# Splitting a norm by token halves between two matmul stages of a decoder layer

## The reference

```
h = h + mod[:, 1, 2] * (merged @ w_out)
u = rms_norm(h, gn[2]) * (1 + scale) + shift
h = h + 0.5 * mod[:, 2, 2] * ((silu(gate(u)) * val(u)) @ w_ffn2_down)
```

## Time and profile before

| | us |
|---|---|
| median of 3 runs | 1338.77 |
| lowest, highest | 1338.13, 1339.8 |
| the profiled execution's own time | 1338.71 |
| its span, first to last instruction | 1336.9 |
| PE busy | 1307.4 (98%) |
| DVE busy | 807.5 (60%) |
| ACT busy | 560.5 (42%) |
| POOL busy | 130.3 (10%) |
| mean granted TensorE clock | 0.994 of full speed |

### The profile page before, as it was taken

How to read it: one execution, slowest core, us unless ns; L and a number is a source line. 1 busy time by engine, 2 the same in 40 slices (tenths; PEclk the granted TensorE clock), 3 DMA queues, 4 the chain that set the end, 5 groups by cost and what they waited for, 6 DMA issues and landing times.

```text
span 1336.9 us, 26512 instructions
## 1 busy us (share of the span) xinstructions
PE 1307.4 (98%) x10448; PEld 1219.0 (91%) x10448; DVE 807.5 (60%) x1665; ACT 560.5 (42%) x1101; POOL 130.3 (10%) x144
## 2 busy tenths in 40 slices
PE   7899999999999999999999999999999999999997
PEld 5698888999999989999898687899899999999997
DVE  4549686789622254446546645553698888973334
ACT  1255454566511143223236545542466555651213
POOL 2320000000011120000003210033300000001110
PEclk9899999999999999999999999999999999999999
DMA  9922877322344346354572221073123222233332
GB/s 341 367 104 64 286 261 252 114 98 95 112 154 153 90 170 199 114 185 134 143 262 88 95 73 39 25 214 111 48 80 110 96 95 96 95 109 88 87 86 78
DMA packets 98772, 180.90 MB, mean 135 GB/s; under 512 B 14005, under 2 KB 49461, under 8 KB 97502
## 3 DMA queue, kind: packets, MB, share of 16 engines
q1 hardware_dynamic: 89734, 163.81, 38.0%
q10 hardware_dynamic: 8920, 15.46, 3.2%
HBM read 173.11 MB, written 10.28 MB: 137 GB/s over the span
## 4 chain that ended last, share of the span: by engine, by line
PE 87%; SPq 4%; DVE 3%; DMA 2%; issue 2%; ACT 1%; ACTq 1%; POOL 0%; DVEq 0%; POOLq 0%
PE PS L2405 31%; PE PS L2481 31%; PE PS L2791 7%; PE PS L2437 3%; PE PS L2292 3%; PE PS L2805 2%; PE PS L2354 2%; PE PS L2817 2%; PE PS L2833 2%; SPq L838 1%; PE PS L2600 1%; DMA raw<-in_w_gu 1%; ACTq L1037 1%; DMA raw<-in_w_in 1%; DMA ch<-in_cmp_pages 1%
## 5 line engine op out<-in xcount | busy, mean ns | idle before, releaser
L2481 PE MATMUL PS<-X,wh 128*128 128x272 f32 x2240 | 428.2, 290 | 1.3 <-DVE wl L1672 0.8
L2481 PEld LDWEIGHTS PS<-X,wh 128*128 128x128 f32 x2240 | 352.0, 188 | 16.3 <-issue 12.7
L2481 PE MATMUL PS<-X,wl 128*128 128x272 f32 x1120 | 324.2, 289 | 0.0
L1566 DVE TENSOR_TENSOR wl<-raw,wh 128x1024 fp32r<-128x1024 f32 (+3 forms) x127 | 133.7, 1054 | 237.4 <-ACT wh L1086 237.1
L1086 ACT ACTIVATE wh<-raw 128x1024 fp32r<-128x1024 f32 (+3 forms) x125 | 110.1, 882 | 349.8 <-PE PS L2405 330.1
L2481 PEld LDWEIGHTS PS<-X,wl 128*128 128x128 f32 x1120 | 210.7, 188 | 0.0
L2405 PE MATMUL PS<-hl,wh 128*128 128x272 f32 x660 | 136.1, 288 | 0.0
L1149 ACT ACTIVATE wh<-S 128x512 fp32r<-128x512 f32 x160 | 100.5, 628 | 63.9 <-DVE S L1691 34.6
L1672 DVE TENSOR_TENSOR wl<-S,wh 128x512 fp32r<-128x512 f32 x160 | 109.9, 687 | 26.6 <-ACT wh L1149 26.3
L2405 PEld LDWEIGHTS PS<-hl,wh 128*128 128x128 f32 x660 | 103.6, 188 | 0.0
L2405 PE MATMUL PS<-X,wh 128*128 128x272 f32 x518 | 102.1, 288 | 0.0
(11 more groups left out here) (386 smaller groups left out, 2360.2 us busy)
## 6 DMA issues: line engine op xcount, KB each, us to landing
raw<-in_w_gu SPq DMA_DIRECT2D x88, 512.0 KB, 4.3
ada<-in_w_ada SPq DMA_DIRECT2D x24, 1024.0 KB, 5.5
raw<-in_w_in SPq DMA_DIRECT2D x39, 512.0 KB, 4.2
raw<-in_w_dn SPq DMA_DIRECT2D x32, 384.0 KB, 3.2
raw<-in_w_dn SPq DMA_DIRECT2D x32, 320.0 KB, 2.9
ada<-in_w_ada ACTq DMA_DIRECT2D x8, 1024.0 KB, 11.4
ch<-in_cmp_pages SPq DMA_DIRECT2D x56, 128.0 KB, 6.3
kv<-in_sel_pages SPq DMA_DIRECT2D x112, 64.0 KB, 1.9
```

Of the source, the lines that this page charges most:

```text
L1566: e.tensor_tensor(wl[:, u % SPLITS, 0:n, :], raw[:, u % RAWS, 0:n, :], f(wh[:, u % SPLITS, 0:n, :]), ALU.subtract).then_inc(lo_ready, 1)
L2481: ins = mm(triple(i, PASS_BANK[j]), w[:, k, :], X[:, s, part, k, :], start=(j in (A11, A12, S1) and k == 0 and w is wh_ and part == 0), st ...
```

## The change: what it does

- Output tiles 6 and 7 run by halves: 6 a=0, 7 a=0, 6 a=1, 7 a=1, 24 matmuls each. DVE adds each half to `h` when it is done (`residual_half`); POOL squares tile 6 by halves, ACT tile 7.
- The norm's sum, root, diagonal and spread exist once per half. The first half's sums stand on PE inside tile 6's second half (before k=4), its spread inside tile 7's second half (before k=2).
- The pair of gate units takes all eight k of half 0, then all of half 1, and waits for `u_lo` before each. Half 1's sums stand behind k=1 of half 0, its spread behind k=4; the eight `ada_step`s follow k=2 to 7 of half 0.
- The pair's weights go to tiles of their own, `wh_ahead` and `wl_ahead`, split by ACT and DVE ahead of the norm. Unit ug+2 is split whole, at the norm's end, and no longer in two parts.
- Semaphore counts behind the norm are shifted. SP's list is as it was.

The diff, cut to its core:

```diff
-PAIRS = (U_GU1, U_WIN, U_CO, U_GU2)
+PAIRS = (U_GU1, U_WIN, U_CO)
...
+        s8 = ExitStack()
+        sb(s8, "in_use_8", [P, 4 * T])
+        wh_ahead = sb(s8, "wh_ahead", [P, 2, 8, P], F32R)
+        wl_ahead = sb(s8, "wl_ahead", [P, 2, 8, P], F32R)
+        s8.close()
...
-                with e.Fori(0, KD - 1) as k:
+                with e.Fori(0, KD - 2 if n == 2 else KD - 1) as k:
...
+                if n == 2:
+                    for a in range(2):
+                        e.wait_ge(h_ready, 2 * KD - 1 + 2 * a)
+                        e.wait_ge(ssq_ready, 23 + a)
+                        e.tensor_tensor(sq[:, side(a)], h[:, KD - 2, side(a)], h[:, KD - 2, side(a)], ALU.mult
+                                        ).then_inc(sq_ready, 1)
+                        e.wait_ge(sq_ready, 21 + a)
+                        e.tensor_tensor(ssq[:, side(a)], ssq[:, side(a)], sq[:, side(a)], ALU.add).then_inc(ssq_ready, 1)
...
+            def split_ahead(u):
+
+                e.wait_ge(raw_in[u % RAWS], 16 * (u // RAWS + 1))
+                e.wait_ge(unit_used, U_OUT)
+                e.activation(wh_ahead[:, u - U_GU2, :, :], raw[:, u % RAWS, :, :], ACT.Copy).then_inc(hi_ready, 1)
+
+            def norm_halves():
+
+                def squared(a):
+                    e.wait_ge(h_ready, 16 + 2 * a)
+                    e.activation(rinv[:, side(a)], h[:, KD - 1, side(a)], ACT.Square).then_inc(sq_last, 1)
+
+                def rooted(a):
+                    e.wait_ge(ms_ready, 3 + a)
+                    e.activation(root5[:, 3 * a:3 * a + 3], root5[:, 3 * a:3 * a + 3], ACT.Sqrt).then_inc(root_ready, 1)
+
+                def modulated(a, k):
+                    e.wait_ge(nt_ready, 16 + KD * a + k + 1)
+                    t0, t1 = HT * a, TP if a else HT
+                    e.activation(normed(2, k)[:, t0:t1], normed(2, k)[:, t0:t1], ACT.Identity,
+                                 scale=mods[:, 48 + 8 + k, 0:1], bias=mods[:, 48 + k, 0:1]).then_inc(nt_mod, 1)
+
+                def rounded(a, k):
+                    e.wait_ge(nt_mod, 16 + KD * a + k + 1)
+                    if a:
+                        e.wait_ge(ns_mod, 16 + k + 1)
+                    e.activation(X[:, x_set(k, a), 0, k % 4, :], normed(2, k)[:, side(a)], ACT.Copy).then_inc(u_hi, 1)
+
+                squared(0)
+                rooted(0)
+                e.wait_ge(mods_ready, 3)
+                for a in range(2):
+                    for k in range(KD):
+                        modulated(a, k)
+                        if k == 0:
+                            rounded(a, 0)
+                        elif k > 1:
+                            rounded(a, k - 1)
+                        if (a, k) == (0, 2):
+                            squared(1)
+                        elif (a, k) == (0, 3):
+                            rooted(1)
+                    rounded(a, KD - 1)
+                u = U_GU2 + 2
+                e.wait_ge(raw_in[u % RAWS], 16 * (u // RAWS + 1))
+                e.wait_ge(unit_used, U_OUT + KD - 1)
+                e.activation(wh[:, u % SPLITS, :, :], raw[:, u % RAWS, :, :], ACT.Copy).then_inc(hi_ready, 1)
...
-                split_second(ug + 2)
+                if n == 0:
+                    split_second(ug + 2)
...
-                split(u)
+                if u < U_GU2:
+                    split(u)
+                else:
+                    split_ahead(u)
...
-            norm(2)
+            norm_halves()
...
+            def norm_halves():
+
+                def lo_ahead(u):
+                    e.wait_ge(hi_ready, u + 1)
+                    e.tensor_tensor(wl_ahead[:, u - U_GU2, :, :], raw[:, u % RAWS, :, :], f(wh_ahead[:, u - U_GU2, :, :]),
+                                    ALU.subtract).then_inc(lo_ready, 1)
+
+                def residual_half(m, a):
+                    o = PS[:, 2 * (m % 4) + a, 0:HT]
+                    gm = mods[:, 24 + 16 + m, :]
+                    if a == 0:
+                        e.wait_ge(half_used, m - KD + 3)
+                        e.scalar_tensor_tensor(out=h[:, m, 0:HT], in0=o, scalar=gm[:, 0:1], in1=h[:, m, 0:HT],
+                                               op0=ALU.mult, op1=ALU.add).then_inc(h_ready, 1)
+                        return
+                    e.wait_ge(unit_used, U_OUT + m + 1)
+                    e.scalar_tensor_tensor(out=h[:, m, HT:TP], in0=o[:, 0:PA], scalar=gm[:, 0:1], in1=h[:, m, HT:TP],
+                                           op0=ALU.mult, op1=ALU.add)
+                    e.tensor_tensor(sres[:, :].rearrange("p (b q) -> p b q", b=NB),
+                                    o[:, PA:HT].rearrange("p (b q) -> p b q", b=NB),
+                                    gm[:, 1:NMOD].unsqueeze(2).broadcast_to([P, NB, SQ]), ALU.mult).then_inc(psum_free, 1)
+                    e.wait_ge(psum_free, O_OUT + m + 1)
+                    e.tensor_tensor(h[:, m, TP:T], h[:, m, TP:T], sres[:, :], ALU.add).then_inc(h_ready, 1)
+                    e.wait_ge(h_ready, 2 * KD + m - KD + 3)
+
+                def factors(a):
+                    r3 = root5[:, 3 * a:3 * a + 3]
+                    e.wait_ge(ssum_ready, 3 + a)
+                    e.tensor_scalar(r3, PS[:, 4, 4 * a:4 * a + 3], 1.0 / D, EPS, ALU.mult, ALU.add).then_inc(ms_ready, 1)
+                    e.wait_ge(root_ready, 3 + a)
+                    e.reciprocal(r3, r3).then_inc(rinv_ready, 1)
+                    e.wait_ge(rinv_ready, 3 + a)
+                    e.tensor_tensor(rinv[:, HT * a:HT * a + 2 * P].rearrange("p (t q) -> p t q", t=2),
+                                    ident.unsqueeze(1).broadcast_to([P, 2, P]),
+                                    r3[:, 0:2].unsqueeze(2).broadcast_to([P, 2, P]), ALU.mult)
+                    e.tensor_scalar(rinv[:, HT * a + 2 * P:HT * a + HT], ident[:, 3 * P - HT:P], r3[:, 2:3], None, ALU.mult
+                                    ).then_inc(diag_ready, 1)
+
+                def scaled(a, k):
+                    if k == 0:
+                        e.wait_ge(spread_ready, 5 + a)
+                    e.tensor_tensor(normed(2, k)[:, side(a)], h[:, k, side(a)], PS[:, 6 + a, 0:HT], ALU.mult
+                                    ).then_inc(nt_ready, 1)
+
+                def low(a, k):
+                    e.wait_ge(u_hi, 16 + KD * a + k + 1)
+                    s = x_set(k, a)
+                    e.tensor_tensor(X[:, s, 1, k % 4, :], normed(2, k)[:, side(a)], f(X[:, s, 0, k % 4, :]), ALU.subtract
+                                    ).then_inc(u_lo, 1)
+
+                lo_ahead(U_GU2)
+                residual_half(KD - 2, 0)
+                lo_ahead(U_GU2 + 1)
+                residual_half(KD - 1, 0)
+                factors(0)
+                residual_half(KD - 2, 1)
+                for a in range(2):
+                    scaled(a, 0)
+                    scaled(a, 1)
+                    for k in range(KD):
+                        if k + 2 < KD:
+                            scaled(a, k + 2)
+                        if (a, k) == (0, 1):
+                            residual_half(KD - 1, 1)
+                        elif (a, k) == (0, 3):
+                            factors(1)
+                        low(a, k)
+                lo(U_GU2 + 2)
...
-            for m in range(KD):
-                if m < KD - 1:
-                    lo(U_OUT + m + 2)
+            for m in range(KD - 2):
+                lo(U_OUT + m + 2)
                 e.wait_ge(unit_used, U_OUT + m + 1)
                 residual(m, 0, 24 + 16, m % 4, O_OUT, KD)
-            lo(U_OUT + KD + 1)
-            norm(2)
+            norm_halves()
...
+            def norm_halves():
+
+                def sums(tile, a, first):
+                    for t, c in enumerate((0, P, HT - P)):
+                        ins = mm(PS[:, 4, 4 * a + t:4 * a + t + 1], tile[:, HT * a + c:HT * a + c + P], ones[:, 0:1],
+                                 start=(first and t == 0), stop=not first, skip_group_check=True)
+                    return ins
+
+                def squares_summed(a):
+                    e.wait_ge(ssq_ready, 24 + a)
+                    sums(ssq, a, True)
+                    e.wait_ge(sq_last, 3 + a)
+                    sums(rinv, a, False).then_inc(ssum_ready, 1)
+
+                def spread(a):
+                    e.wait_ge(diag_ready, 5 + a)
+                    mm(PS[:, 6 + a, 0:HT], ones[:, :], rinv[:, side(a)], start=True, stop=True).then_inc(spread_ready, 1)
+
+                def output_half(m, a, at):
+                    u = U_OUT + m
+                    if a == 0:
+                        e.wait_ge(lo_ready, u + 1)
+                        e.wait_ge(psum_free, O_OUT + m - 3)
+                    for k in range(KD):
+                        if k in at:
+                            at[k](0)
+                        for w, x in ((wh, mh), (wh, ml), (wl, mh)):
+                            ins = mm(PS[:, 2 * (m % 4) + a, 0:HT], w[:, u % SPLITS, k, :], x[:, k, side(a)],
```

(85 more changed lines are left out.)

29 lines of the change are left out of this document (15 added, 14 removed).

## The result

The changed kernel takes 1342.03 us (median of 13 runs, 1340.35 to 1344.76) against 1338.73 for the kernel before, run beside it (13 runs, 1336.48 to 1340.31): ratio 1.0027, interval 1.0019 to 1.0035. It is slower by 3.3 us. The forecast was +0.7, in the class "within 0.2%", with 1341.9 as the upper end. The profiled execution took 1342.66, with a span of 1340.9 (before: 1336.9) and a mean granted clock of 0.992 (before: 0.994).

A forecast was written before the change was run, and what follows sets the result against it. PE was taken as the bound, so only its standing still around the third norm could be won. Stalls 3.4 against 2.6 (+0.8), sums +0.5, Strassen gap -0.6: net +0.7 us, 1339.4, range 1337.4 to 1341.9.

The forecast's parts named there:

- The collision and the stall: Before the first half's sums: DVE's subtractions and POOL's squares and additions block each other, so PE stands still 2.2 us.
- all three hand-overs: Between DVE and POOL before `ssq`: second begins 0.14 before the first ends; by the skill's figure each is 0.25 us later.
- The mixture in the pair: In the pair of gate units: 64 rows of `ada_step` priced about 4.0 us, wide matmuls 0.75 per k.
- The pair's waits: PE's waits: 0.1 at the pair's first k, 0.8 at k=1, 0.2 at k=3, 0.1 behind the last k.
- The sums: One-column sums of the norm: 24 rows for 20, +0.5 us of PE work.
- The gap in the Strassen part: Behind unit ug+3: PE's wait for DVE's product L1785, 0.4 us or 0.6 by turns, disappears: -0.6.
- POOL is not in the way: Rival, before the first sums: `ssq` ready at 942.8, first stall only 0.4, 1.8 less, 1337.6 us; chance 0.12.
- everything hides: Rival: all PE's stalls (2.6 + 0.6) are won, less 0.5 for sums: 1336.0 us at best; chance 0.03.
- The samples on POOL hold the second half: Rival, pair's second half: ACT's rounding waits for POOL's operations, PE loses time, +2.5, in all 1341.9 us; chance 0.12.

The follow-up runs named there:

- the filled kernel: Sixteen wide matmuls with unread results put on PE ahead of the wait for the first half's squares, on the changed kernel: 1340.61 us, ratio 1.0017.
- the runs with four groups instead of six: The eight `ada_step`s in four pairs, their sum copied before the split, on the kernel with tile 5's residual first and sums one k later: 1337.30 us, ratio 0.9984.
- the one with two groups: The changed kernel with its eight `ada_step`s in two groups of four, behind k=2 and k=3: 1342.74 us, ratio 1.0034.
- that with stall and sums apart: The changed kernel with the wait for the squares left at k=4 and the first half's sums moved to k=7: 1343.30 us, ratio 1.0031.
- the kernel with later sums: The changed kernel with tile 5's residual ahead of tile 7's weight split and the first half's sums one k later: 1337.82 us, ratio 0.9991.

## Why the prediction was wrong, point by point

- **The collision and the stall: right.** Forecast 2.2 us from 942.4 to 944.6, measured 2.21, ending at 943.58, with tile 6 starting 1.1 earlier; square and addition 1.96 and 2.21, half square .64, all as forecast. POOL's square ends at 939.62 and takes 1.09 alone, so it began at 938.53, 0.14 before DVE's subtraction ended (937.44 + 1.23 = 938.67), the same hand-over as in the earlier trace rows. The Trainium skill's figure ("SBUF — State Buffer", the section "A bandwidth-pool intuition that's wrong (but worth ruling out)") has the loser begin some 115 ns after DVE's end. The prediction put it on all three hand-overs, but only in two of them does POOL wait for DVE; by the page's figure, an estimate, the stall would have been 0.5 longer, about 2.7. This trace does not agree with it.
- **The step that failed: a stall was priced at its own length.** The prediction counted the 2.2 us and then let PE go on at 0.125 a matmul. In the run PE came back at half clock: the 12 sums took 2.72 instead of the 1.50 of the filled kernel, the 18 wide matmuls behind them 4.16 instead of some 2.35: **3.0 us** more in this profile, as much as the filler won back in D (1.4 between the medians). No rival had this. The trace of before had no such place around the norm: there the clock stayed at 1.00, with waits of .4, .8 and 1.0. But it had one near its start, and I did not look there: PE stands still for 4.92 us, and the work behind the wait runs at half clock up to 58.5 (PE by stretches, before):

```profile
47.70:52.60 4.90, 0.03 (x1) 0.56 0.98 318
52.60:58.50 5.90, 5.85 (x26) 0.50 1.05 373
```

That wait is twice as long as this stall. It shows that a wait has a second price, not from what length on. In the last norm, with waits of .7 and 1.3, the clock fell too, but only at 1331.6, behind PE's last matmul, where it costs nothing.
- **The mixture in the pair: a term that was left out.** "64 rows of `ada_step` about 4.0 us" and "PE needs 0.75 per k" were true of each kind alone. Alternating, each k behind an `ada_step` takes .95 instead of .75 (six times, 1.2), the k behind the sums .86 (0.1), the two k behind a wait 1.00 and 1.02 (0.5), and the `ada_step`s 4.28 instead of 4.0, a single one .57 instead of .50 (0.3): some 2.1 us in all. The runs with four groups instead of six (.69 less) agree; the earlier trace rows had these matmuls only behind one another.
- **The pair's waits: over-sized.** Forecast .1, .8, .2 and .1, measured .21, .33, 0 and 0: 0.7 less. The half clock is not the reason: the filled kernel, at full clock, has .20 and .34. At the second k the chain through the residual is as long as forecast, but PE's first k started later and took longer, and so less of it is seen as a wait. Some 0.3 us is only the way of counting: the trace counts a wait from the end of the last record, .13 to .16 behind its turn, and the forecast counted from the turn. The later waits are gone because the mixture gave DVE and ACT more lead; that is argued from the waits of .26 and .61 that came back with fewer groups.
- **The sums:** forecast +0.5 for four more rows; 1.50 + 1.23 against the 2.49 of before is +0.25 at full clock.
- **The gap in the Strassen part: right in kind, under-sized.** Forecast -0.6. The part took 211.87 for 1680 matmuls, against 1194.17 - 981.34 = 212.83 before: -0.96.
- **The rivals.** *POOL is not in the way* and *everything hides* did not happen. *The samples on POOL hold the second half* did not happen either: POOL's sample operations took .24 to .48 and PE waits for nothing in the second half. It named a time near the measured one, 1341.9, for a reason that is not there.

From +0.7: -0.7 (waits), -0.25 (sums), -0.36 (gap), +3.0 (clock), +2.1 (mixture) makes +4.5, of +4.53 by D. The share of the clock differs from one execution to the next (3.0 in this profile, 1.6 in the one with two groups), so the medians need not carry the same sum, and they do not: they are 3.3 apart. Open is what decides between a held and a lost clock at waits near half a microsecond, and for how long it is lost.

## What to carry to other kernels

Price a stall of TensorE twice: its length, and what the work behind it costs at half clock, and look for places in the trace of before where the clock already falls behind a wait. Before work of DVE is moved into an idle stretch, look at what POOL does there; here moving one residual ahead of a split, and the sums three matmuls later, turned the same change from +3.3 us to about -1.2. Then ask what the repair alone is worth: the same move in the kernel before, without the halves, gave as much (ratio 0.9989 against 0.9991). Small matmuls used as filler have a price at each return to the wide ones, so put them in few groups, but not so few that the engines behind lose their lead.

## What was not expected of the hardware

- The clock fell behind a stall of 2.20 to 2.21 us in three kernels, and behind .50 and .73 followed by one-column sums in two; it held with .24, .35 (three kernels) and .49. The kernel before kept it with .95 between wide matmuls, and lost it at its start with 4.92. So the length of the wait alone does not decide it.
- The half clock lasted about 3.4 us in three profiles, 6.8 in the changed kernel's and some 10 in that with stall and sums apart. It began within 0.3 us of PE's return in two of the kernels with the long stall and 2.1 us later in the third.
- A return from the `ada_step`s, fp32 matmuls with weights of 32 columns, to the wide ones costs about 0.2 us of TensorE's time, six times in the changed kernel's profile (.94 to .96 for a k against .75); a return from the one-column sums costs 0.1 (.86).
- DVE's and POOL's operations hold each other up in turn, in both directions: 2.12 and 1.96 for a 1.23 subtraction, 1.95, 2.22 and 1.44 for POOL's 1.09, 1.36 and .64, where two subtractions and three of POOL's operations meet (the kernel with later sums).
